# A four-mixer trunk on one core: the loads and the S5 setup of the first pass rearranged

## What is computed

```python
for l in range(2):
    h = rmsnorm(x, norm_w[l])
    proj = einsum('bld,de->ble', h, w_in[l])
    (s5_x, s5_g, hg_q, hg_f, hg_i, hg_g, ml_q, ml_k, ml_v, ml_o,
     ml_i, ml_f, ml_g, rt_q, rt_k, rt_v, rt_g) = split(proj)
    s5_out = s5_mixer(s5_x, ...)       # a_bar = exp(lam*dt), b_bar, complex diagonal state
    ho = chunked_gated_recurrence(silu(hg_q), ...)   # HGRN
    mh = mlstm_chunked(ml_q, ml_k, ml_v, ml_i, ml_f, ...)
    ro = chunked_gated_recurrence(rotary(rt_q), rotary(rt_k), rt_v, ...)  # retention
    x = x + concat(gated outputs) @ w_out[l]
y = rmsnorm(x, final_norm_w)
```

## Time and profile before

| | |
|---|---|
| median of three runs | 1521.51 us (1521.27 to 1527.04) |
| the profiled execution | 1528.97 us |
| its span | 1527.2 us |
| TensorE (PE) busy | 1368.9 us, 90% |
| VectorE (DVE) busy | 817.1 us, 54% |
| ScalarE (ACT) busy | 654.5 us, 43% |
| GpSimd (POOL) busy | 198.5 us, 13% |
| granted TensorE clock, mean | 0.937 |
| chain that ended last | PE 61%, DVE 13%, ACT 9%, DMA 8%, issue 5%, SPq 3% |
| SP's first DMA issue | 0.72 us |

### The profile page before, as it was taken

One profiled execution on the slowest core, in us unless ns is written; L12 is line 12 of the kernel. 1 busy time (PEld: TensorE's weight loads), 2 busy tenths in 40 slices (PEclk: granted clock), 3 DMA queues, 4 the chain that ended last, 5 costly groups with the idle time before them and its releaser, 6 DMA issues.

```text
span 1527.2 us, 31412 instructions
## 1 busy us (share of the span) xinstructions
PE 1368.9 (90%) x12391; PEld 1202.6 (79%) x12391; DVE 817.1 (54%) x2670; ACT 654.5 (43%) x1309; POOL 198.5 (13%) x292
## 2 busy tenths in 40 slices
PE   3979999898897999988999899979998899889896
PEld 2878888787777988877778898869877888778665
DVE  5966464544984336545355525455366325634546
ACT  5665544454245444334532464445532644421011
POOL 3101112110001111111000211220000121211001
PEclk9988999899999999988999999989999899889888
DMA  7855547363248565565513675746335557754501
GB/s 204 186 153 136 141 113 219 97 183 85 74 137 217 130 160 128 123 159 125 145 54 117 170 190 127 209 115 177 83 108 141 117 137 179 207 107 98 147 10 60
DMA packets 183690, 208.68 MB, mean 137 GB/s; under 512 B 65233, under 2 KB 157145, under 8 KB 181881
## 3 DMA queue, kind: packets, MB, share of 16 engines
q0 software_dynamic: 16128, 58.86, 19.9%
q1 hardware_dynamic: 96696, 76.38, 18.0%
q10 hardware_dynamic: 70720, 71.44, 15.6%
HBM read 124.42 MB, written 23.37 MB: 97 GB/s over the span
## 4 chain that ended last, share of the span: by engine, by line
PE 61%; DVE 13%; ACT 9%; DMA 8%; issue 5%; SPq 3%; POOL 1%; ACTq 0%; DVEq 0%; POOLq 0%
PE psum L2407 16%; PE psum L2405 16%; PE psum L2736 5%; PE psum L2714 3%; DMA wraw<-in_w_in 2%; PE psum L2655 2%; DVE r L2111 2%; PE psum L2566 2%; DMA ud<-r 2%; DVE r L1737 2%; PE psum L2474 2%; ACT whi L1246 1%; ACT wlo L1244 1%; PE psum L2654 1%; ACT r L1518 1%
## 5 line engine op out<-in xcount | busy, mean ns | idle before, releaser
L2407 PE MATMUL psum<-whi,hhi 128*128 128x256 f32 (+1 forms) x896 | 259.9, 299 | 13.0 <-ACT th L1334 5.6
L2407 PE MATMUL psum<-whi,hlo 128*128 128x256 f32 (+1 forms) x896 | 251.8, 290 | 0.0
L2407 PE MATMUL psum<-wlo,hhi 128*128 128x256 f32 (+1 forms) x896 | 227.8, 290 | 7.2 <-DMA wlo<-wraw 7.2
L2405 PE MATMUL psum<-hhi,whi 128*128 128x288 f32 (+2 forms) x672 | 227.6, 344 | 1.9 <-DVE hlo L1712 1.5
L2405 PE MATMUL psum<-hlo,whi 128*128 128x288 f32 (+2 forms) x672 | 216.0, 327 | 0.0
L2407 PEld LDWEIGHTS psum<-whi,hhi 128*128 128x128 f32 x896 | 177.5, 198 | 16.1 <-issue 12.2
L2405 PE MATMUL psum<-hhi,wlo 128*128 128x288 f32 (+2 forms) x672 | 188.0, 324 | 0.0
L2407 PEld LDWEIGHTS psum<-whi,hlo 128*128 128x128 f32 x896 | 177.9, 199 | 3.2 <-issue 3.0
L2736 PE MATMUL psum<-wraw,mixT 128*128 128x256 f32 x768 | 174.7, 387 | 3.3 <-DVE xo L2328 3.3
L2407 PEld LDWEIGHTS psum<-wlo,hhi 128*128 128x128 f32 x896 | 161.6, 196 | 8.5 <-DMA wlo<-wraw 8.0
L1200 POOL DMA_DIRECT2D wlo<-wraw x112 | 99.5, 912 | 514.0 <-ACT wlo L1244 509.3
(11 more groups left out here) (356 smaller groups left out, 2313.9 us busy)
## 6 DMA issues: line engine op xcount, KB each, us to landing
wlo<-wraw POOLq DMA_DIRECT2D x104, 512.0 KB, 8.1
wraw<-in_w_in ACTq DMA_DIRECT2D x50, 1024.0 KB, 6.9
...
r<-x SPq DMA_DIRECT2D x10, 512.0 KB, 8.5
...
```

What stands on the lines that cost most here:

```text
L2405: mm = nc.tensor.matmul(bank.t[:, 0:ln], wv[:, kt, k[2] * P:(k[2] + 1) * P], x[:, kt, c0:c0 + ln], start=first, stop=last)
L2407: mm = nc.tensor.matmul(bank.t[:, 0:width], x[:, kt, k[2] * P:k[2] * P + P], wv[:, kt, :], start=first, stop=last)
```

## The change

- **Loads.** SP issues x tile 0 first, then the identity alone (a part of the constants), the norm weights, x tiles 1 to 3, the first two weight blocks and then the other constants. In pass 0 the four tiles have places of their own (`tslot`). The eight parameter loads move from SP's queue to ScalarE's. TensorE waits for the identity at first, and for the rest of the constants at its first projection piece.
- **POOL's setup** loses the clearing of mixT and hq2 before `pool_setup`; behind it, 16 partitions of four rows of mixT and hq2 are cleared, with a signal `pool_zero` for those who need it.
- **Parameters.** The five transposes of the parameters come behind the transposes of tile 0, their evictions on ScalarE (`parameters`) behind the square of tile 1, and p, p2, p3, e, e2 behind the norm, among the first projection pieces. The small lb work moves from the start of VectorE and ScalarE into steps p and p2.
- **The first weight split** stands behind tile 2's eviction instead of tile 1's.
- **The later setup.** e3, b, A0, AX and A1 of chunk 0 stand among the hg_i, hg_q and hg_g pieces. va, vb, wa, wb, t0 to t3, k0, k1 and s move behind the opening: into the ml_ifg pieces and the first HGRN chunks. The resulting order is given below.
- **mq and mvv** are cleared by POOL at the first ml_q piece of each pass instead of by VectorE at the first ml_ifg piece; ifc and mgate go to the end of R2 (10,280 columns now), so that ml_ifg can be evicted while the setup's buffers are in use; ScalarE takes over the waits that this needs.

The diff, cut to its core:

```diff
-    first = norm(0)
-    if "s5" in parts:
-        first = first[:3] + [(("s5set", 0), "p")] + first[3:] + [(("s5set", 0), "p2"), (("s5set", 0), "p3")]
-    plan = first + spread(opening, s5set(0)[:8]) + head[:1] + s5set(0)[8:12] + head[1:k] + s5set(0)[12:]
+    parameters = [(("s5set", 0), x) for x in ("p", "p2", "p3")] + s5set(0)[:4] if "s5" in parts else []
+    plan = placed("open", 0, norm(0) + opening, parameters + head[:k], None)
     head = head[k:]
+    rest = project(0, "ml")
+    gates = [x for x in rest if x[1][1][1] == "ml_ifg"]
+    rest = [x for x in rest if x not in gates]
+    if "s5" in parts:
+        m = s5set(0)[4:]
+        gates = gates[:3] + m[:1] + gates[3:5] + m[1:2] + gates[5:] + m[2:]
...
-            b = filler + project(n, "ml")
+            b = filler + (project(n, "ml") if n else gates + rest)
...
+    ("open", 0): (8, 9, 10, 10, 10, 24, 26, 31, 34, 34),
-    ("hg", 0): (5, 5, 5, 8, 8, 11, 11, 13, 13, 14, 14, 14, 17, 17, 17, 22, 23, 23, 23, 25, 25, 26, 26, 29, 29, 30, 30, 30, 30, 33, 33, 33, 33, 34, 34, 35),
+    ("hg", 0): (0, 0, 0, 1, 1, 1, 6, 7, 8, 9, 9, 11, 12, 12, 14, 14, 15, 15, 17, 17, 19, 19, 19, 19, 19, 19, 19, 19, 20, 20, 20, 20, 20, 20, 21, 21, 21, 21, 27, 27, 28, 37, 39, 39, 40, 40, 41, 42),
-    ("ml", 0): (1, 3, 4, 4, 6, 8, 8, 8, 8, 8, 8, 10, 10, 12, 12, 13, 13, 15, 15, 16, 16, 16),
+    ("ml", 0): (1, 3, 5, 6, 6, 6, 8, 8, 9, 9, 11, 12, 12, 13, 13, 15, 15, 15, 15, 19, 22, 26),
...
-        tslot = {k: k[1] % NCH if k in norm_tiles and k[0] else k[1] % 2 for k in all_tiles}
+        tslot = {k: k[1] % NCH if k in norm_tiles else k[1] % 2 for k in all_tiles}
...
-        mvv, mo, mgate = R2.take(5, 4, 65), R2.take(5, 256), R2.take(5, 256)
-        ifc = R2.take(5, 8)
+        mvv, mo = R2.take(5, 4, 65), R2.take(5, 256)
...
+        R2.at = R2.size - 1320
+        ifc, mgate = R2.take(5, 8), R2.take(5, 256)
...
             if s[0] == "norm":
-                return part == 1 and s[1] == 0
+                return part == 2 and s[1] == 0
...
             load_x((0, 0))
+            sp.dma_start(ident, inp["c_packed"][:, 0:P]).then_inc(*ident_in.inc("ident"))
+            norm_weights(0)
+            for t in range(1, NCH):
+                load_x((0, t))
+            for k in w_loads[:2]:
+                src, width = weight_columns(k)
+                sp.dma_start(weights(wraw, wslot[k], width), src.rearrange("(k p) c -> p k c", p=P)).then_inc(*wr_in[wslot[k]].inc(k))
+            sp.dma_start(const[:, P:], inp["c_packed"][:, P:]).then_inc(*const_in.inc("packed"))
...
-            for v, x in ((epow[:, :], -0.5), (ST[:, :, :], 0.0), (STs[:, :, :], 0.0), (ssq[:, :], 0.0), (ssq_rest[:, :], 0.0), (mixT[:, :, :], 0.0), (hq2[:, :, :], 0.0), (D32[:, :, :], 0.0)):
+            for v, x in ((epow[:, :], -0.5), (ST[:, :, :], 0.0), (STs[:, :, :], 0.0), (ssq[:, :], 0.0), (ssq_rest[:, :], 0.0), (D32[:, :, :], 0.0)):
...
+            nc.gpsimd.memset(mixT[0:16, 0:4, :], 0.0).then_inc(*pool_zero.inc("mixT"))
+            nc.gpsimd.memset(hq2[:, :, :], 0.0).then_inc(*pool_zero.inc("hq2"))
...
             for s, part in plan:
+                if s[0] == "proj" and part == ("mm", pieces_of_block(s[1], "ml_q")[0]):
+                    n = s[1]
+                    if n:
+                        pool.wait_ge(*y_done.at([m for m in mixes if m[1] < n and m[0] == "ml"][-1]))
+                        pool.wait_ge(*s5_dve.at(("s5", n - 1, "mixed")))
+                    if s5n and n < 2:
+                        pool.wait_ge(*set_out.at(("s5set", n, 10)))
+                    nc.gpsimd.memset(mq, 0.0).then_inc(*pool_done.inc())
+                    nc.gpsimd.memset(mvv[:, :, :, 64:65], 1.0).then_inc(*ml_clear.inc(n))
...
                     square_sum((s[1], part))
+                    if (s[1], part) == (0, 1):
+                        parameters()
...
                     if name == "ml_ifg":
-                        act.wait_ge(*ml_clear.at(n))
+                        if n:
+                            act.wait_ge(*s5_dve.at(("s5", n - 1, "mixed")))
+                            act.wait_ge(*y_done.at([m for m in mixes if m[1] < n and m[0] == "ml"][-1]))
+                        if n == 1:
+                            act.wait_ge(*set_out.at(("s5set", 1, 10)))
...
-                    if part[1] == pieces_of_block(n, "ml_ifg")[0]:
-                        if n:
-                            dve.wait_ge(*y_done.at([m for m in mixes if m[1] < n and m[0] == "ml"][-1]))
-                        if s5n and n < 2:
-                            dve.wait_ge(*set_out.at(("s5set", n, 10)))
-                        nc.vector.memset(mq, 0.0).then_inc(*dve_done.inc())
-                        nc.vector.memset(mvv[:, :, :, 64:65], 1.0).then_inc(*ml_clear.inc(n))
```

More of the change, by code:

```diff
@@ L658, in tile_rows @@
             if tslot[k] == 2:
-                return mixT[:, 2:4, 0:HALF] if k[0] % 2 == 0 else mixT[:, 8:10, 0:HALF]
+                return mixT[:, 2:4, 0:HALF] if k[0] == 2 else mixT[:, 8:10, 0:HALF]
             return two[min(tslot[k], 2)]
@@ L765, in trunk_kernel @@
         pool_setup = signal("pool_setup", ["all"])
+        pool_zero = signal("pool_zero", ["mixT", "hq2"])
         lb_exp = signal("lb_exp", ["in"])
@@ L978, in _ @@
                                          ).then_inc(*set_in.inc(s + (4 * ri + 2 + d,)))
+                    if l == 0:
+                        sp.wait_ge(*pool_zero.at("mixT"))
                     for t in range(1, 8) if l == 0 else ():
@@ L1058, in _ @@
                     n = s[1]
-                    if n == 0 and part and part + 1 in tiles_of(n):
-                        load_x((n, part + 1))
                     if n and part == 0 and NCH in tiles_of(n):
@@ L1797, in _ @@
                     if part == "p2":
+                        dve.wait_ge(*lb_exp.at("in"))
+                        nc.vector.tensor_tensor(mx, lb[:, 4:6], lb[:, 6:8], ALU.add).then_inc(*dve_done.inc())
+                        settle()
+                        nc.vector.reciprocal(mx, mx).then_inc(*dve_done.inc())
+                        settle()
+                        dve.wait_ge(*const_in.at("packed"))
+                        dve.wait_ge(*small_in.at("b_f"))
+                        nc.vector.tensor_copy(cm[:, :], cm_wide).then_inc(*dve_done.inc())
+                        nc.vector.tensor_tensor(lb[:, 0:2], lb[:, 6:8], mx, ALU.mult).then_inc(*dve_done.inc())
+                        nc.vector.tensor_tensor(lb[:, 2:4], lb[:, 4:6], mx, ALU.mult).then_inc(*lb_done.inc("all"))
+                        dve.wait_ge(*lb_done.at("all"))
                         ts(XX, XX, 1 / 128, None, ALU.mult)
@@ L2370, in _ @@
                             mm.then_inc(*bank.full.inc(u))
+                    if s[1:] == (0,) and part == 0:
+                        pe.wait_ge(*dt_rows.at("wide"))
+                        for k, (rows_, at_) in enumerate(((16, 0), (16, 16), (16, 32), (4, 48), (4, 52))):
+                            mm = nc.tensor.transpose(aux.t[:, at_:at_ + rows_], param_rows[0:rows_, k, :], ident[0:rows_, 0:rows_])
+                        mm.then_inc(*aux.full.inc(("params", -1)))
                 elif s[0] == "proj" and part[0] in ("mm", "mm2"):
+                    if part == ("mm", pieces[0]):
+                        pe.wait_ge(*const_in.at("packed"))
                     b, n = s[1:], s[1]
```

83 lines of the change are left out of this document (34 added, 49 removed).

## The result

The changed kernel is slower: 1540.97 us (median of 4, 1536.62 to 1544.21) against 1524.05 us for the kernel before, run beside it (median of 4), a ratio of 1.012 (95% interval 1.0094 to 1.0146). That is 17 us; the forecast was 10, from 1521.51 to 1531 us. The profiled execution took 1538.38 us, its span is 1536.5 us, the mean granted clock 0.937 as before.

The account below looks back on a forecast made before the run. The setup moved behind the opening, with t0 waiting for wb, was to become the bound: 8.4 us gained at the start, more TensorE idling later, first mLSTM chunk 10 us later, so 1521.51 becomes 1531 us, range 1510 to 1541.

Parts of the forecast that it names:

- rival A: The forecast itself: the setup moved behind the opening becomes the bound; 1525 to 1541 us, chance 0.5.
- (2): HGRN projection: VectorE's setup parts and hg_q's eviction let A0 start at 70.7 us, 15.5 us earlier than before.
- (6): Stretch to the first mLSTM chunk, at 199.7 against 189.7 us; ledger 21 us more idle, less 8.4 and 2 to 3.
- (1): Loads at the start: first projection matmul at 25.5 us instead of 33.87, a gain of 8.4 us (4.9 to 9.9).
- (4): Moved setup parts on VectorE: 36.6 us, wb ends at 123.9; TensorE idles 6.6 us before C(0), 13 before t0.
- (3): The mixer's first chunk: AX holds ScalarE until 80.5 us, so TensorE idles 4.2 us before ml_ifg piece 0.
- (5): Behind wb: POOL's clear waits for Tm stores until 144 us; TensorE idles 3.5 us for ml_k's low halves (0 to 8.1).
- (7): Everything else, such as parameter loads, smaller POOL setup and passes 1 to 3: 0 us.
- B: The setup hides under the mixer if wb ends before about 88 us after the first projection matmul; 1513 us, chance 0.24.
- C: A wash: t0 waits, but POOL's clear is in time and gaps overlap, (3) and (5) shrink to 0; 1523 us, chance 0.16.
- D: Loads at the start do less, giving 5 us only, later gaps unchanged; 1535 us, chance 0.1.

Follow-up runs that it names:

- early_setup: The changed kernel with every S5 setup part back in the opening in the earlier order, new loads kept; 1524.2 us, 0.9996 of the kernel before.
- dve_more: early_setup with 30 repeats of one small VectorE multiply added in setup part p2; 1529.0 us, 1.0045 of the kernel before.
- a0_first: early_setup with A0(0) ahead of setup part wb and AX two pieces later; 1521.3 us, 0.9985 of the kernel before.
- zero_after_em: The changed kernel with the 14 zero stores into Tm behind the Em store on SP's queue; 1537.0 us, 1.008 of the kernel before.
- low_first: The changed kernel with POOL computing ml_k's low halves ahead of the clear of mq; 1539.9 us, 1.0104 of the kernel before.
- zero_late: The changed kernel with the zero stores into Tm moved in plan order only, still issued at 21.59 us; 1543.6 us, 1.012 of the kernel before.
- zero_low: zero_after_em and low_first in one, on the changed kernel; 1534.2 us, 1.0078 of the kernel before.
- vw_early: The changed kernel with the setup's parts up to wb back in the opening, t and k left among HGRN pieces; 1538.4 us, 1.0112 of the kernel before.
- after_fill: The changed kernel with only ml_q to ml_o at their earlier places, or right behind k1 where later; 1534.6 us, 1.0093 of the kernel before.
- tk_early: vw_early with t0 to t3, k0 and k1 moved from HGRN chunk 2 to beside chunk 0; 1537.5 us, 1.0085 of the kernel before.
- tk_fill: tk_early with the ml_q to ml_o pieces at the places of the kernel before; 1521.0 us, 0.9977 of the kernel before.

## Why the prediction was right and wrong

The direction and the place of the loss (rival A, t0's wait for wb) were right, the size was too small: the first mLSTM chunk was forecast 10 us later and came 17.8 later, and the medians moved by 16.9. Two terms failed: the time of hg_q's load in (2), and the price of the lower clock in the ledger of (6). The chunk is 7.8 us later than forecast. Along the path 0.6 of this is the start, 4.0 come between the first projection matmul and t0, and 3.2 behind t0. The ledger in (6) splits the same 7.8 us another way, by idle and busy time.

- **(1) Start:** first projection matmul 26.12, forecast 25.5. Right. The price of 8.4 us for it was booked as a gain of TensorE. What it is worth alone is nothing measurable (early_setup): VectorE's work counts up to C(0) (dve_more), with the chain of t and k beside it (a0_first). In the forecast's path this did no harm, for it followed VectorE through (2) to (4).
- **(2) A0(0) near 70.7: measured 74.96. This step failed.** It took hg_q's split to be ready when TensorE was, and (1) had left the zero stores, which now start at 21.77 instead of 25.02 us, out of the count. While they are in flight hg_q's load takes 13.0 us, 10.0 without them. That is 2.4 us of the way from the first matmul to A0(0) by zero_after_em, 3.0 us at the first mLSTM chunk. Another 0.6 is the start; 1.3 of the 4.3 remain unaccounted.
- **(3), (4) The gaps:** 4.08, 5.70 and 12.62 us for 4.2, 6.6 and 13. The stretch from ml_ifg 0's gate to the end of wb took 38.1 us for 36.6 (the forecast's own terms, without waits, add up to 37.4). It began 2.9 us late, and wb ended at 128.4 instead of 123.9.
- **(5) Behind wb: the size was about right, the path to it was not.** The clear came 5.9 us late (149.88 for 144), of which 4.6 is t0. The forecast priced the wait of ml_k's matmuls for their low halves (3.5 us). That wait was 0.67 us; the cost came by the load of ml_o, which ScalarE may issue only when these halves have landed and which took 10.5 us, so that an eviction was late and TensorE waited 2.64 us more. Together 3.3 us, and low_first, where both waits are gone, gives 3.9 at the first mLSTM chunk. That two different waits agree in size is luck.
- **(6) The ledger by gaps: this term failed.** It had 37 us of idle time; measured are 35.4 (181.41 - 145.99), so the idle time is not what was missed. It then took off 2 to 3 us for stretches at half clock that move. Measured is the opposite sign: the same matmuls were busy 6.0 us longer, at a mean granted clock of 0.90 for 0.93. 19.6 us of new idle time and 6.0 of busy time less 7.75 at the start are the 17.8. Two places are easy to see: t0 to t3, behind the wait of 12.62 us, were busy 3.9 us for 2.1 before; and ml_v's last two pieces, behind the wait of 2.64 us, took 7.46 us at a granted clock of 0.77, where two such pieces took 5.95 at 1.00 before. How much of the 3.2 us behind t0 is the clock's was not tried by a run and stays open.
- **(7) Everything else 0:** the mark moved by 17.8 us, the medians by 16.9. It held, as far as that can be told: in the two profiles the part behind the mark is 8.5 us shorter in the changed kernel (1329.0 for 1337.5), but it is 1339.4 in zero_late, which runs as the changed kernel does.
- **The rivals:** B (hidden) needed wb before s + 88; it ended at s + 102. C needed the gap of (3) to go; it was 4.08. D needed a start gain of 5 us; it was 7.75. The measured median lies on the upper edge of the stated range, 1541, by 0.03 us; that it is not outside is luck too.

Taking away both late loads (zero_low) moves the chunk from 207.53 to 199.29, but 3.5 us of these 8.2 were in the forecast already. So both loads explain 4.7 of the 7.8 us by this run, or 3.4 by the single runs (zero_after_em 3.0, low_first 3.9 less 3.5). The other 3 to 4 us have no run that isolates them.

What the forecast didn't see as a cause, though its sum contained it: the loss has three links, wb late, then t and k late, then the ml pieces behind k1. Mending the first alone gives 0 us (vw_early), the last alone 2.1 (after_fill), the first two 5.0 (tk_early), all three 18.9 (tk_fill, 188.6 for 207.5).
